# A hybrid decoder layer on one core: GELU moved to VectorE and ScalarE, memory fills one unit earlier, w_out multiplied by branch halves, every other sort step written backwards

## The chip, the cores and the metric

One core of a Trainium2 chip. The metric is device time in microseconds, the median of several runs. TensorE is called PE, VectorE DVE, ScalarE ACT, GpSimd POOL and SyncE SP, as in the profile.

## The reference, cut to what matters

A layer on 512 tokens of width 1024, all in float32. Its first part is what the change touches:

```
z = rmsnorm(h) @ W_in                     # -> u_ssm | q | k | v, 512 columns each
y = S5(u_ssm) + d_skip * u_ssm;  y = gelu(y)          # tanh form
y_ssm = rmsnorm(y * sigmoid(y @ w_glu)) * g_ssm
y_att = rmsnorm_per_head(differential attention of q, k, v: 4 heads, causal)
h = h + concat(y_ssm, y_att) @ W_out
h = h + CrossAttn(rmsnorm(h), rmsnorm(mem))           # 256 memory tokens
h = h + MoE(rmsnorm(h))                               # 64 experts, top 8, and a shared one
return rmsnorm(h)
```

## The kernel before, in words

The program is written by engine: each engine has its own list in order, and semaphores join them. Tokens are four tiles of 128 (`NT`). PSUM has eight banks of 128x512.

*Differential attention* runs in 16 units `u` (`NU`), query tile `u // 4` and head `u % 4`; a unit has `u // 4 + 1` key tiles. PE runs `turn_weights(u)` (L950, transposes of the weights), `scores(u + 2)` (L940), a fill if there is one, and `values(u)` (L960). DVE runs `weights(u)` (reciprocal, L1883, and the scalar_tensor_tensor L1886 that combines the two softmaxes) and `row_max(u + 2)` (mask add, L1874). ACT runs `exps(u + 1)` (L1425), the copy of the turned weights (L1452), and after each fourth unit `outputs` (squares and a copy of the four heads). Scores have two pairs of banks (0 to 3), turned weights banks 4 and 5, outputs bank 6, fills bank 7.

*Fills.* Keys and values of the cross-attention memory come from 16 small products. Four run ahead of the S5 output; `fill(0)` to `fill(11)` stand in units 0 to 11, each 16 matmul instructions of 256 columns (L896 keys, L909 values), evicted by `mem_out` on ACT in the next unit (L1403, L1407). `fill(4)` and `fill(8)` each begin new weight blocks.

*GELU* runs on POOL (L2260 to L2267) on all four tiles at once, 128x2048: two steps for y + d_skip u, three for the inner polynomial, then ACT's tanh in unit 10 (`TANH_AT`, L1449), then two more steps. When the units are over, PE turns the GELU (L992, 16 transposes), ACT evicts (L1459), PE multiplies by w_glu (L766, `dense`), ACT takes the sigmoid (L1462), DVE multiplies (L1608), ACT squares and takes the root, DVE scales (L1915), PE turns both branches together (L747), ACT and DVE evict with the gains (L1311, L1660), and PE multiplies by w_out in two column halves of two row blocks each. DVE adds the result to h (L1611, `residual`).

*Weights* outside the experts are 1 MB blocks in the three buffers `dw`, loaded by SP in the order of `blocks`; block i waits until block i - 3 is used up (`release`). Experts 0 and 1, three blocks of 1 MB each, are queued on SP behind the second block of wq_x.

*The sort.* `slot_table` draws an expert's row numbers, eight at a time, in 16 steps of MAX8 and MATCH_REPLACE8 on 64 partitions, and writes them with a stride of four into groups of 32 slots. A slot is a partition of the gathers and scatters in the expert stage; an empty one moves nothing.

## Time and profile before

| what | value |
|---|---|
| median of 3 runs | 1190.99 us (1184.29 to 1196.14) |
| profiled execution | 1187.29 us |
| its span | 1185.5 us, 13271 instructions |
| PE busy | 1096.1 us, 92% |
| DVE, ACT, POOL busy | 391.1, 232.0, 147.6 us |
| granted PE clock over the span | 0.967 of full speed |

Durations come from this one execution. A line number is one of the kernel before. A matmul in float32 is recorded as two instructions, so a block product of 16 matmuls is counted as x32. A time in brackets is the idle time of the engine before the row, with what ended it.

### The profile page before, as it was taken

How to read it: one execution, taken by the hardware profiler on the slowest of the kernel's cores; microseconds unless marked ns; L12 is line 12 of the kernel's file. 1: busy time of each engine (PE TensorE's matmuls, PEld its weight loads, DVE VectorE, ACT ScalarE, POOL GpSimd, SP SyncE). 2: the span in 40 equal slices, each digit the busy share in tenths (PEclk: the TensorE clock that was granted, in tenths of full speed). 3: DMA queues.
4: the chain of work that ended last, by engine and by line, in shares of the span. 5: the costliest groups of instructions: out<-in, count | busy, mean ns of one | idle time of the engine just before them, and what ended most of it. 6: DMA issues, size and time to landing. Idle time of an engine off the chain costs nothing.

```text
span 1185.5 us, 13271 instructions
## 1 busy us (share of the span) xinstructions
PE 1096.1 (92%) x5059; PEld 527.9 (45%) x5059; DVE 391.1 (33%) x899; ACT 232.0 (20%) x525; POOL 147.6 (12%) x194
## 2 busy tenths in 40 slices
PE   7999797977799987999999999999899999999996
PEld 4444585754444454444444443333234334443332
DVE  1983565353202012016932222212122121111147
ACT  3311432334202023003101111111011111111142
POOL 3000005120000000000022121221121212121100
PEclk9999798988899998999999999999899999999998
DMA  7225322212127240223469999999999999999996
GB/s 217 99 71 106 67 103 50 77 65 71 36 71 283 72 177 1 68 71 132 192 245 413 421 421 420 420 421 420 421 420 421 419 422 419 421 420 419 413 418 258
DMA packets 77346, 298.82 MB, mean 252 GB/s; under 512 B 20342, under 2 KB 23707, under 8 KB 50652
## 3 DMA queue, kind: packets, MB, share of 16 engines
q1 hardware_dynamic: 64386, 264.29, 56.8%
q0 software_dynamic: 12672, 33.57, 7.2%
q8 instruction: 42, 0.69, 0.2%
q14 instruction: 28, 0.23, 0.1%
q10 hardware_dynamic: 218, 0.04, 0.0%
HBM read 280.04 MB, written 27.39 MB: 259 GB/s over the span
## 4 chain that ended last, share of the span: by engine, by line
PE 84%; DVE 8%; DMA 4%; ACT 3%; issue 1%; SPq 0%; DVEq 0%; POOL 0%; POOLq 0%
PE ps L1167 26%; PE ps L766 26%; PE ps L1183 13%; PE ps L1149 4%; PE ps L896 2%; PE ps L909 2%; DMA dw<-expert_rows 2%; PE ps L747 2%; PE ps L1048 1%; PE ps L1024 1%; PE ps L1191 1%; DVE z L2059 1%; DVE z L1886 1%; PE ps L940 1%; DVE z L2056 1%
## 5 line engine op out<-in xcount | busy, mean ns | idle before, releaser
L1167 PE MATMUL ps<-ring,z 128*32 128x512 f32 (+2 forms) x1056 | 285.7, 597 | 1.0 <-DVE z L2107 1.0
L766 PE MATMUL ps<-dw,act_t 128*128 128x512 f32 x576 | 250.3, 595 | 1.8 <-ACT act_t L1311 0.9
L766 PEld LDWEIGHTS ps<-dw,act_t 128*128 128x128 f32 x576 | 109.4, 191 | 137.9 <-issue 136.4
L1183 PE MATMUL ps<-ring,act_t 128*32 128x512 f32 (+2 forms) x528 | 145.3, 596 | 0.9 <-DVE act_t L2132 0.9
L1167 PEld LDWEIGHTS ps<-ring,z 128*32 128x32 f32 (+2 forms) x1056 | 90.3, 131 | 111.0 <-issue 108.7
L1167 PE MATMUL ps<-dw,z 128*64 128x512 f32 (+2 forms) x256 | 99.0, 594 | 0.3 <-DVE z L2107 0.3
L1167 PE MATMUL ps<-z 128*32 128x512 f32 (+2 forms) x288 | 87.8, 628 | 4.0 <-issue 4.0
L1540 ACT ACTIVATE tok<-ps 128x256 f32<-128x256 f32 x44 | 16.9, 384 | 305.4 <-PE ps L1167 305.4
L2087 DVE COPY z<-ps 128x512 f32<-128x512 f32 x44 | 30.5, 692 | 117.6 <-PE ps L1183 117.6
L1183 PEld LDWEIGHTS ps<-ring,act_t 128*32 128x32 f32 (+2 forms) x528 | 43.4, 131 | 49.2 <-issue 47.0
L2273 POOL COPY ixb<-tabs 128x1 uint32<-128x1 uint32 x88 | 17.1, 194 | 376.2 <-DVE z L2087 362.9
L1608 DVE TENSOR_TENSOR tok<-tok,ps 128x256 f32<-128x256 f32 x22 | 9.3, 422 | 156.3 <-ACT tok L1540 156.3
L1608 DVE TENSOR_TENSOR act_t<-tok,ps 128x256 f32<-128x256 f32 x22 | 9.3, 422 | 148.1 <-ACT tok L1540 148.1
L766 PE MATMUL ps<-act_t,dw 128*128 128x512 f32 x128 | 55.2, 593 | 0.9 <-ACT act_t L1311 0.9
L1183 PE MATMUL ps<-act_t 128*64 128x512 f32 (+2 forms) x128 | 50.9, 597 | 2.8 <-issue 2.8
L1536 ACT ACTIVATE z<-ps 128x512 f32<-128x512 f32 x44 | 26.3, 597 | 134.3 <-PE ps L1183 134.3
L1611 DVE TENSOR_TENSOR h<-h,ps 128x512 f32<-128x512 f32 x24 | 16.2, 686 | 103.6 <-PE ps L766 101.0
L2317 POOL DMA_INDIRECT expert_rows<-z,ixb x44 | 44.8, 1018 | 36.8 <-POOL ixb L2273 34.5
L1167 PEld LDWEIGHTS ps<-z 128*32 128x32 f32 (+2 forms) x288 | 26.7, 133 | 42.4 <-issue 41.6
L1183 PE MATMUL ps<-dw,act_t 128*32 128x512 f32 (+2 forms) x144 | 43.6, 596 | 0.0
L1149 PEld LDWEIGHTS ps<-cst,tok 128*128 128x128 f32 x264 | 32.6, 193 | 24.3 <-issue 24.3
L1167 PEld LDWEIGHTS ps<-dw,z 128*64 128x64 f32 (+2 forms) x256 | 28.9, 130 | 28.2 <-issue 27.6
(327 smaller groups left out, 1251.0 us busy)
## 6 DMA issues: line engine op xcount, KB each, us to landing
ring<-in_w_gate SPq DMA_DIRECT2D x42, 1024.0 KB
ring<-in_w_up SPq DMA_DIRECT2D x42, 1024.0 KB
ring<-in_w_down SPq DMA_DIRECT2D x42, 1024.0 KB, 28.3
dw<-in_w_gate SPq DMA_DIRECT2D x11, 1024.0 KB
dw<-in_w_up SPq DMA_DIRECT2D x11, 1024.0 KB
act_t<-in_w_down SPq DMA_DIRECT2D x11, 1024.0 KB, 28.9
z<-in_w_gate SPq DMA_DIRECT2D x11, 1024.0 KB, 22.8
z<-in_w_up SPq DMA_DIRECT2D x11, 1024.0 KB, 26.9
```

The lines of the kernel that those rows point to most:

```text
L747: ins = pe.transpose(ps[:, c, i * P:(i + 1) * P], src[:, i, c * P:(c + 1) * P], ident)
L766: ins = pe.matmul(ps[0:m, bank0 + j, 0:n], lhs(w, q * 4 + c4, c4, j), rhs(w, q * 4 + c4, c4, j), start=(q == 0 and c4 == 0), stop=(q == le ...
L896: ins = pe.matmul(ps[:, bank, 0:MEM], w4(dw[:, i % 3, :])[:, c4, j * P:(j + 1) * P], memt[:, hf * 4 + c4, :], start=(hf == 0 and c4 == 0), ...
L909: ins = pe.matmul(ps[:, bank, 0:256], memt[:, hf * 4 + c4, m * P:(m + 1) * P], w4(dw[:, i % 3, :])[:, c4, n * 256:(n + 1) * 256], start=(h ...
L1149: ins = pe.transpose(ps[:, c // 4, (c % 4) * P:(c % 4 + 1) * P], xg[r % 4][:, c:D:NC_D], ident)
L1167: ins = pe.matmul(ps[rows, 2 + r % 2, :], xtt[r % 2][:, c, rows], ring_wgu(BUF[x])[:, :, c, :], start=(c == 0), stop=(c == NC_D - 1))
L1183: ins = pe.matmul(ps[rows, 5 + n, :], htt[r % 2][:, c, rows], ring_wd(BUF[x])[:, c, n * 512:(n + 1) * 512], start=(c == 0), stop=(c == 1))
L1536: act.activation(yo[j % 2][:, 0:512], ps[:, 5, :], ACT.Copy).then_inc(e_yea, 1)
L1608: return dve.tensor_tensor(o, a, b, ALU.mult)
L2087: dve.tensor_copy(yo[j % 2][:, 512:D], ps[:, 6, :]).then_inc(e_yev, 1)
L2273: pool.tensor_copy(ixb[:, b:b + 1], tabs[:, which, col:col + 1] if isinstance(col, int) else tabs[:, which, bass.ds(col, 1)]).then_inc(s_p ...
L2317: pool.indirect_dma_start(yr, bass.IndirectOffsetOnAxis(ap=ixb[:, b:b + 1], axis=0), yo[r % 2], None, bounds_check=last_row, oob_is_err=Fa ...
```

## The change

GELU leaves POOL. DVE computes y + d_skip u tile by tile in units 2 to 5 (`gelu_input`), ACT squares it (units 3 to 6), DVE forms the inner product (units 5 to 8), ACT takes tanh (units 6 to 9), DVE forms twice the GELU (units 7 to 10). PE turns it in four steps in units 11 to 14 by way of bank 7 (`turn_gelu`), ACT evicts with the factor 0.5 behind each. `fill(0)` runs before unit 0, `fill(u + 1)` in unit u. The w_out blocks are ordered by branch: attention rows first, both column halves, then the SSM rows. The attention half is turned and multiplied without waiting for the SSM norm; the SSM half is turned unnormalized, and 1/rms, one number per token, is applied when its product is added to h. Each of the four block products ends in a semaphore step of its own, and a weight block is released when it ends. In `slot_table` each odd step writes its eight values in the opposite order. POOL's `s_gst` steps in the expert stage use another semaphore.

```diff
@@ -48,7 +48,7 @@
 LAMBDA0 = 0.8 - 0.6 * math.exp(0.0)
 BIG = 1e30
 K_EARLY = 4
-TANH_AT = 10
+GELU_SQUARE_AT, GELU_TANH_AT, GELU_TURN_AT = 3, 6, 16 - K_EARLY - 1
 GELU_C = math.sqrt(2.0 / math.pi)
 TWO_PI = 2.0 * math.pi
@@ -298,7 +298,10 @@
     half_blocks("wv_x", 2)
     blocks.append(("w_glu", 0, 0, [(lambda v: v.rearrange("p (c n) -> p c n", c=4),
                                     t["w_glu"][0].rearrange("(c p) n -> p c n", p=P))]))
-    half_blocks("w_out", 2)
+    for part, rows in enumerate((slice(SW, D), slice(0, SW))):
+        for cb in range(2):
+            src = t["w_out"][0][rows, cb * 512:(cb + 1) * 512].rearrange("(c p) n -> p c n", p=P)
+            blocks.append(("w_out", part, cb, [(lambda v: v.rearrange("p (c n) -> p c n", c=4), src)]))
     half_blocks("wq_x", 2)
     half_blocks("wo_x", 2)
     for hf in range(2):
...
@@ -456,7 +459,7 @@
     for name, cb, hf, _ in blocks:
         if name in ("wk_x", "wv_x"):
             release.append((s_kv, 4 * cb + (8 if name == "wv_x" else 0) + 4))
-        elif hf == 0 and (name, cb, 1) in index:
+        elif name != "w_out" and hf == 0 and (name, cb, 1) in index:
             firsts += 1
             release.append((dw_half, firsts))
         else:
@@ -976,37 +979,65 @@
         scores(1)
         pe.wait_ge(s_yea, 2)
         pe.wait_ge(s_yev, 2)
+        def turn_gelu(c):
+            if c == 0:
+                pe.wait_ge(s_kve, 16)
+                pe.wait_ge(s_yg, NT)
+            else:
+                pe.wait_ge(s_yge, c)
+            for i in range(NT):
+                ins = pe.transpose(ps[:, 7, i * P:(i + 1) * P], gl[0][:, i, c * P:(c + 1) * P], ident)
+            ins.then_inc(s_ygt, 1)
+        fill(0)
         for u in range(NU):
             turn_weights(u)
             if u + 2 < NU:
                 scores(u + 2)
-            if u < 16 - K_EARLY:
-                fill(u)
+            if u + 1 < 16 - K_EARLY:
+                fill(u + 1)
+            elif u - GELU_TURN_AT < 4:
+                turn_gelu(u - GELU_TURN_AT)
             values(u)
-        pe.wait_ge(s_yg, 1)
-        pe.wait_ge(s_e, 2 * NU)
-        for c in range(4):
-            for i in range(NT):
-                ins = pe.transpose(ps[:, c, i * P:(i + 1) * P], gl[0][:, i, c * P:(c + 1) * P], ident)
-            ins.then_inc(s_ygt, 1)
         pe.wait_ge(s_yge, 4)
         pe.wait_ge(s_wte, NU)
-        pe.wait_ge(s_oe, NT)
-        dense([("w_glu", 0, 0)], 4, NT, lambda w, c, c4, j: ygt[:, c, j * P:(j + 1) * P], weight_rhs, s_gl)
+        dense([("w_glu", 0, 0)], 4, NT, lambda w, c, c4, j: ygt[:, c, j * P:(j + 1) * P], weight_rhs, s_gl,
+              bank_waits=[[], [], [(s_oe, NT)], []])
+        def turn_half(bank0, src, ready):
+            for c in range(4):
+                for i in range(NT):
+                    if c == 0:
+                        pe.wait_ge(ready, i + 1)
+                    ins = pe.transpose(ps[:, bank0 + c, i * P:(i + 1) * P], src[:, i, c * P:(c + 1) * P], ident)
+                ins.then_inc(s_tf, 1)
+        def out_part(part, cb, bank0, bank_waits=()):
+            dense([("w_out", part, cb)], bank0, NT, lambda w, c, c4, j: at3[:, 4 * (1 - part) + c4, j * P:(j + 1) * P],
+                  weight_rhs, s_wo, bank_waits=bank_waits)
+        pe.wait_ge(s_e, 2 * NU)
+        turn_half(0, tok3[:, :, SW:D], s_cat)
+        pe.wait_ge(s_tea, 6)
+        pe.wait_ge(s_tev, 6)
+        out_part(0, 0, 0)
         pe.wait_ge(s_sg, NT)
-        pe.wait_ge(s_kve, 16)
-        turn(s_tf, NT, tok3, lambda c, i: [(s_cat, i + 1)] if c == 0 else [])
+        turn_half(4, gl[2], s_y3)
+        out_part(0, 1, 0, [[(s_h1, j + 1)] for j in range(NT)])
         pe.wait_ge(s_tea, 8)
         pe.wait_ge(s_tev, 8)
-        for cb in range(2):
-            dense([("w_out", cb, 0), ("w_out", cb, 1)], 4 * cb, NT, tokens_lhs, weight_rhs, s_wo)
-        turn(s_tf, NT, h, lambda c, i: [(s_h1, c + 4)] if c % 4 == 0 and i == 0 else [])
+        out_part(1, 0, 0, [[(s_h1, NT + j + 1)] for j in range(NT)])
+        out_part(1, 1, 4)
+        turn(s_tf, NT, h, lambda c, i: [(s_h1, 12 + c)] if c % 4 == 0 and i == 0 else [])
         pe.wait_ge(s_tea, 12)
         pe.wait_ge(s_tev, 12)
         for cb in range(2):
@@ -1438,35 +1469,50 @@
         exps(0)
         for u in range(NU):
-            if 1 <= u <= 16 - K_EARLY:
-                mem_out(K_EARLY + u - 1, 7)
             if u + 1 < NU:
                 exps(u + 1)
+            if u < 16 - K_EARLY:
+                mem_out(K_EARLY + u, 7)
             if u % HEADS == 0 and u:
                 outputs(u // HEADS - 1)
-            if u == TANH_AT:
-                act.wait_ge(s_gin, 1)
-                act.activation(gl[2], gl[1], ACT.Tanh, scale=GELU_C).then_inc(s_th, 1)
+            if 0 <= u - GELU_SQUARE_AT < NT:
+                i = u - GELU_SQUARE_AT
+                act.wait_ge(s_gin, i + 1)
+                act.activation(gl[1][:, i, :], gl[0][:, i, :], ACT.Square, scale=math.sqrt(0.044715)).then_inc(s_gst, 1)
+            if 0 <= u - GELU_TANH_AT < NT:
+                i = u - GELU_TANH_AT
+                act.wait_ge(s_gin, NT + i + 1)
+                act.activation(gl[2][:, i, :], gl[1][:, i, :], ACT.Tanh, scale=GELU_C).then_inc(s_th, 1)
             act.wait_ge(s_wtf, u + 1)
             n = (u // HEADS + 1) * P
             act.activation(wt[:, u % 2, 0:u // HEADS + 1, :],
                            ps[:, 4 + u % 2, 0:n].rearrange("p (j q) -> p j q", q=P), ACT.Copy).then_inc(s_wte, 1)
+            if 0 <= u - GELU_TURN_AT < 4:
+                c = u - GELU_TURN_AT
+                act.wait_ge(s_ygt, c + 1)
+                act.activation(ygt[:, c, :], ps[:, 7, :], ACT.Copy, scale=0.5).then_inc(s_yge, 1)
         outputs(NT - 1)
         roots(3, slice(16, 32), slice(68, 84))
-        for c in range(4):
-            act.wait_ge(s_ygt, c + 1)
-            act.activation(ygt[:, c, :], ps[:, c, :], ACT.Copy).then_inc(s_yge, 1)
         for i in range(NT):
             act.wait_ge(s_gl, i + 1)
             act.activation(gl[1][:, i, :], ps[:, 4 + i, :], ACT.Sigmoid).then_inc(s_sg, 1)
+        act.wait_ge(s_pce, 2)
+        def turned_half(first, bank0, chunk0):
+            for c in range(0, 4, 2):
+                act.wait_ge(s_tf, first + c + 1)
+                act.activation(at3[:, chunk0 + c, :], ps[:, bank0 + c, :], ACT.Copy, scale=gcat[:, chunk0 + c:chunk0 + c + 1]
+                               ).then_inc(s_tea, 1)
+        turned_half(8, 0, 4)
         squares(0, NT, gl[2], gl[3], SW, [[(s_y3, i + 1)] for i in range(NT)])
+        turned_half(12, 4, 0)
         roots(4, slice(0, NT), slice(8, 8 + NT))
-        act.wait_ge(s_pce, 2)
-        turned(8, gcat, S, at3)
         turned(16, pcol[:, R_GX:R_GX + 8], S, at3)
-        squares(0, NT, h, tok3, D, [[(s_h1, 8)]] + [[]] * 3)
+        squares(0, NT, h, tok3, D, [[(s_h1, 16)]] + [[]] * 3)
         roots(5, slice(0, NT), slice(8, 8 + NT))
         for q in range(0, 8, 2):
             act.wait_ge(s_qx, q + 1)
@@ -1886,12 +1932,35 @@
             dve.scalar_tensor_tensor(out=e[0], in0=e[1], scalar=r, in1=e[0], op0=ALU.mult, op1=ALU.add
                                      ).then_inc(s_w, 1)
+        def gelu_input(i):
+            if i == 0:
+                dve.wait_ge(s_yt, 16 * (2 * NT + 1))
+                dve.wait_ge(s_y, 4)
+            link(mul(gl[0][:, i, :], z3[:, i, 0:SW], dsk))
+            add(gl[0][:, i, :], gl[0][:, i, :], y3[:, i, :]).then_inc(s_gin, 1)
+        def gelu_inner(i):
+            dve.wait_ge(s_gst, i + 1)
+            dve.scalar_tensor_tensor(out=gl[1][:, i, :], in0=gl[1][:, i, :], scalar=1.0, in1=gl[0][:, i, :],
+                                     op0=ALU.add, op1=ALU.mult).then_inc(s_gin, 1)
+        def gelu_twice(i):
+            dve.wait_ge(s_th, i + 1)
+            dve.scalar_tensor_tensor(out=gl[0][:, i, :], in0=gl[2][:, i, :], scalar=1.0, in1=gl[0][:, i, :],
+                                     op0=ALU.add, op1=ALU.mult).then_inc(s_yg, 1)
         row_max(0)
         row_max(1)
         for u in range(NU):
             weights(u)
             if u + 2 < NU:
                 row_max(u + 2)
+            for step, first in ((gelu_input, 2), (gelu_inner, 5), (gelu_twice, 7)):
+                if 0 <= u - first < NT:
+                    step(u - first)
         dve.wait_ge(s_osq, NU)
         r0, rstd2, var = st2[:, 0:16], st2[:, 16:32], st[:, 16:32]
@@ -1903,18 +1972,22 @@
         dve.wait_ge(s_oe, NT)
         for i in range(NT):
             o = tok3[:, i, SW:D].rearrange("p (h d) -> p h d", h=HEADS)
-            mul(o, o, rstd2[:, 4 * i:4 * i + 4].unsqueeze(2).to_broadcast([P, HEADS, P]))
-        dve.wait_ge(s_yg, 1)
+            mul(o, o, rstd2[:, 4 * i:4 * i + 4].unsqueeze(2).to_broadcast([P, HEADS, P])).then_inc(s_cat, 1)
+        dve.wait_ge(s_yg, NT)
         for i in range(NT):
             dve.wait_ge(s_sg, i + 1)
-            mul(gl[2][:, i, :], gl[0][:, i, :], gl[1][:, i, :]).then_inc(s_y3, 1)
-        dve.wait_ge(s_sq, 10)
-        rstd(4, st[:, 0:NT], SW, st[:, 8:8 + NT], st2[:, 0:NT])
-        for i in range(NT):
-            dve.tensor_scalar(tok3[:, i, 0:SW], gl[2][:, i, :], st2[:, i:i + 1], None, ALU.mult).then_inc(s_cat, 1)
-        turned(8, gcat, S, at3)
+            dve.scalar_tensor_tensor(out=gl[2][:, i, :], in0=gl[0][:, i, :], scalar=0.5, in1=gl[1][:, i, :],
+                                     op0=ALU.mult, op1=ALU.mult).then_inc(s_y3, 1)
+        def turned_half(first, bank0, chunk0):
+            for c in range(1, 4, 2):
+                dve.wait_ge(s_tf, first + c + 1)
+                dve.tensor_scalar(at3[:, chunk0 + c, :], ps[:, bank0 + c, :], gcat[:, chunk0 + c:chunk0 + c + 1], None, ALU.mult
+                                  ).then_inc(s_tev, 1)
+        turned_half(8, 0, 4)
         def residual(filled, ready, first=0, bank=lambda n: n):
             for n in range(first, first + 8):
@@ -1923,7 +1996,28 @@
                 dve.wait_ge(filled, n + 1)
                 add(hh, hh, ps[:, bank(n), :]).then_inc(ready, 1)
-        residual(s_wo, s_h1)
+        def attention_part(cb):
+            for i in range(NT):
+                hh = h[:, i, cb * 512:(cb + 1) * 512]
+                dve.wait_ge(s_wo, 4 * cb + i + 1)
+                add(hh, hh, ps[:, i, :]).then_inc(s_h1, 1)
+        attention_part(0)
+        turned_half(12, 4, 0)
+        dve.wait_ge(s_sq, 10)
+        rstd(4, st[:, 0:NT], SW, st[:, 8:8 + NT], st2[:, 0:NT])
+        attention_part(1)
+        for cb in range(2):
+            for i in range(NT):
+                hh = h[:, i, cb * 512:(cb + 1) * 512]
+                dve.wait_ge(s_wo, 8 + 4 * cb + i + 1)
+                if cb == 0:
+                    dve.wait_ge(s_h1, i + 1)
+                else:
+                    dve.wait_ge(s_h1, NT + i + 1)
+                dve.scalar_tensor_tensor(out=hh, in0=ps[:, 4 * cb + i, :], scalar=st2[:, i:i + 1], in1=hh,
+                                         op0=ALU.mult, op1=ALU.add).then_inc(s_h1, 1)
         turned(16, pcol[:, R_GX:R_GX + 8], S, at3)
@@ -2047,13 +2141,14 @@
             for q in range(SLOTS // 8):
                 k, row = divmod(q, 4)
                 eight = ts_[0:NE, k * QW + row:(k + 1) * QW:4]
+                filled = eight if q % 2 == 0 else ts_[0:NE, k * QW + row + QW - 4:k * QW + row - 1:-4]
                 left = tv[0:NE, :] if q else values
                 if between and q in between:
                     shared_hidden(between.index(q))
                 if q == ids_at:
                     dve.wait_ge(s_srf, 1)
                     dve.tensor_copy(eid[:], ps[0:1, 0, 2 * NE:3 * NE]).then_inc(s_tab, 1)
-                link(dve.max(out=eight, in_=left))
+                link(dve.max(out=filled, in_=left))
                 if ids_at is not None and q == 0:
                     dve.wait_ge(s_ord, 1)
                 ins = dve.match_replace(out=tv[0:NE, :], in_to_replace=eight,
@@ -2246,26 +2341,6 @@
         pool.memset(toep, 0.0).then_inc(s_zero, 1)
-        gsteps = [0]
-        def link(ins):
-            gsteps[0] += 1
-            ins.then_inc(s_gst, 1)
-            pool.wait_ge(s_gst, gsteps[0])
-        fg = [v.rearrange("p i d -> p (i d)") for v in gl]
-        pool.wait_ge(s_yt, 16 * (2 * NT + 1))
-        pool.wait_ge(s_y, 4)
-        link(pool.tensor_tensor(gl[0], z3[:, :, 0:SW], dsk.unsqueeze(1).to_broadcast([P, NT, SW]), ALU.mult))
-        link(pool.tensor_tensor(fg[0], fg[0], y3.rearrange("p i d -> p (i d)"), ALU.add))
-        link(pool.tensor_tensor(fg[1], fg[0], fg[0], ALU.mult))
-        link(pool.tensor_scalar(fg[1], fg[1], 0.044715, 1.0, ALU.mult, ALU.add))
-        pool.tensor_tensor(fg[1], fg[1], fg[0], ALU.mult).then_inc(s_gin, 1)
-        pool.wait_ge(s_th, 1)
-        link(pool.tensor_scalar(fg[2], fg[2], 0.5, 0.5, ALU.mult, ALU.add))
-        pool.tensor_tensor(fg[0], fg[0], fg[2], ALU.mult).then_inc(s_yg, 1)
         last_token, last_row = pool.to_reg(S - 1), pool.to_reg(S * TOPK - 1)
         def index_of(b, which, col, n):
...
...
```

## Rows read from the trace of the kernel before

**Rows 1.** Busy time by stage: stretch, us, then each engine's busy us (instructions)

```profile
190.00:272.00 82.00, 66.55 (x318) 50.49 (x318) 42.23 (x60) 28.66 (x105) 25.42 (x7) 0.92 0.21 75
...
595.00:1135.00 540.00, 531.51 (x2848) 213.18 (x2843) 109.79 (x252) 68.85 (x131) 106.94 (x174) 0.99 1.00 412
```

**Rows 2.** Timeline of DVE: start us, us, line, operation

```profile
187.32 0.35 DVE L1886 SCALAR_TENSOR_TENSOR z<-z,st 128x128 f32<-128x128 f32 x1
...
196.44 4.67 DVE L1886 SCALAR_TENSOR_TENSOR z<-z,st 128x128 f32<-128x128 f32 x1
...
253.22 4.96 DVE L1886 SCALAR_TENSOR_TENSOR z<-z,st 128x384 f32<-128x384 f32 x1
```

**Rows 3.** Timeline of POOL

```profile
191.88 4.50 POOL L2260 TENSOR_TENSOR ring<-z 128x2048 f32<-128x2048 f32 x1 [180.65 <-DMA z<-in_d_skip]
...
253.27 4.50 POOL L2267 TENSOR_TENSOR ring<-ring 128x2048 f32<-128x2048 f32 x1
```

**Rows 4.** Timeline of PE in the attention units

```profile
184.99 0.30 PE L950 MATMUL ps<-cst,z 128*128 128x128 f32 x1 [2.72 <-DVE z L1886]
...
201.16 0.48 PE L950 MATMUL ps<-cst,z 128*128 128x128 f32 x1 [5.59 <-DVE z L1886]
...
217.55 1.99 PE L909 MATMUL ps<-dw,ring 128*128 128x256 f32 x8 [2.08 <-DMA dw<-in_wv_x]
...
225.93 3.72 PE L909 MATMUL ps<-dw,ring 128*128 128x256 f32 x16
...
258.24 0.90 PE L950 MATMUL ps<-cst,z 128*128 128x128 f32 x3 [4.01 <-DVE z L1886]
```

**Rows 5.** Finer stretches; PEclk is the granted clock

```profile
186.00:191.00 5.00, 5.00 (x20) 4.24 (x19) 1.50 (x5) 0.02 (x1) 0.00 (x0) 0.74 0.82 186
...
201.00:208.00 7.00, 6.84 (x24) 5.13 (x24) 3.92 (x6) 0.37 (x2) 6.79 (x3) 0.67 0.01 2
...
258.20:266.50 8.30, 8.26 (x29) 5.69 (x30) 2.70 (x5) 0.89 (x3) 0.00 (x0) 0.67 0.00 0
266.50:277.00 10.50, 6.34 (x39) 3.80 (x37) 6.22 (x13) 7.38 (x24) 0.00 (x0) 1.00 0.59 201
277.00:283.00 6.00, 5.22 (x23) 4.82 (x24) 0.31 (x1) 1.00 (x5) 0.00 (x0) 0.53 0.00 0
```

**Rows 6.** The chain of waits in unit 13, which has no fill

```profile
271.13 0.66 PE ps L950 x4
...
273.36 1.22 DVE st L1874
...
274.95 0.76 DVE z L1886
275.75 0.67 PE ps L950 x4
```

**Rows 7.** Timeline of PE from the last unit to w_out

```profile
282.40 2.77 PE L992 MATMUL ps<-cst,ring 128*128 128x128 f32 x16
287.80 15.56 PE L766 MATMUL ps<-dw,ring 128*128 128x512 f32 x32 [2.63 <-ACT ring L1459]
309.63 6.48 PE L747 MATMUL ps<-cst,tok 128*128 128x128 f32 x32 [6.27 <-DVE tok L1915]
317.00 55.17 PE L766 MATMUL ps<-dw,act_t 128*128 128x512 f32 x128 [0.89 <-ACT act_t L1311]
```

**Rows 8.** Timelines of ACT and DVE behind the gate matmuls

```profile
303.40 0.60 ACT L1462 ACTIVATE ring<-ps 128x512 f32<-128x512 f32 x1 [2.84 <-PE ps L766]
...
304.03 0.69 DVE L1608 TENSOR_TENSOR ring<-ring 128x512 f32<-128x512 f32 x1 [2.74 <-ACT ring L1462]
...
315.28 1.62 DVE L1660 TENSOR_SCALAR act_t<-ps,gcat 128x512 f32<-128x512 f32 x2 [0.72 <-PE ps L747]
```

**Rows 9.** DMA issues between 100 and 380 us, median us to landing

```profile
dw<-in_w_out SPq DMA_DIRECT2D x4, 1024.0 KB, 5.2
```

**Rows 10.** Queues, from the page: packets, MB, share of 16 engines

```profile
q0 software_dynamic: 12672, 33.57, 7.2%
```

12 lines of the change are left out of this document (6 added, 6 removed).

## The prediction

> **What bounds the kernel now.** I first read the busy time by stage. From 595 us on TensorE is busy 531.51 of 540 us [rows 1]; the change edits nothing there but the row numbering of the sort, so what happens earlier can only shift this stage. The attention stage, 190 to 272 us, is where something is to be had: PE is busy 66.55 of 82 us at a granted clock of 0.92 [rows 1]. The chain of waits and the timelines say why.
>
> First, VectorE stalls while GpSimd runs the GELU. The 128x128 scalar_tensor_tensor of `weights` takes 0.35 us at 187.32, but 4.67 us at 196.44, and the 128x384 one takes 4.96 us at 253.22 [rows 2]. GpSimd's 4.5 us operations start at 191.88 and 253.27 [rows 3], beside them. PE waits for exactly these: 5.59 us before 201.16 and 4.01 us before 258.24. A third wait, 2.72 us before 184.99, is the first softmax unit's plain latency, with the K/V fill queued behind it [rows 4]. Each wait is followed by matmuls at the low level of the clock: the stretches of 5, 7 and 8.3 us after them ran at 0.74, 0.67 and 0.67 [rows 5]. A fill at full speed is 16 instructions in 3.72 us [rows 4].
>
> Second, the last four units carry no fill and run by latency: turn at 271.13, next at 275.75, 4.62 us apart, of which the row maximum alone is 1.22 [rows 6].
>
> Third, between the last value matmul and cross-attention there are serial steps with PE idle: the GELU turns at 282.40 and their evictions before the gate matmuls at 287.80, then squares, a root, a scaling and turns between the gate's end (287.80+15.56=303.36) and the start of w_out at 317.00, with 6.27 us idle before the turns at 309.63 [rows 7].
>
> **The change, part by part.**
>
> *GELU off GpSimd.* Removed: two PE waits, 5.59+4.01=9.6 us [rows 4], and the slow clock behind them, 7x(1-0.67)+8.3x(1-0.67)=5.0 us [rows 5]. Added on VectorE: per token tile a multiply and an add (units 2 to 5), and two scalar_tensor_tensors (units 5 to 8 and 7 to 10), 16 operations of 128x512 at 0.69 each by the gate product [rows 8], 11 us in all; on ScalarE four squares and four tanhs of 0.6 (the sigmoid, same shape) [rows 8]. They lie ahead of the next unit's `weights` in VectorE's order, so what is queued behind them is PE's next turn. A unit with a fill lasts about 5 us, and the fill now sits ahead of that turn. The widest unit gives the upper end of the loop: 4.62 us from turn to turn with one key tile more than most [rows 6], of which row maximum and `weights` shrink with the key tiles (1.22 and 0.76 at four of them, 0.35 for `weights` at one [rows 2, 6]). With three tiles or two I estimate 3.7 and 3.0 us, with one or two GELU steps (1.4 or 1.5) 4.4 to 5.2, against PE's 4.4 to 5.7 (a 3.72 fill and turn, scores and values); only unit 5, with input and inner product together (2.2), overruns, by 0.4. ScalarE's additions stand ahead of the weight copy that `values` needs, but a 3.72 us fill covers them; if it were gone each would cost 0.6. The input of the first step (y3 and d_skip) landed when GpSimd started, 191.88 [rows 3]; VectorE comes to it at about 196, so no wait. Part: -14.6+0.4 = -14.2.
>
> *Fills forward by one.* Fill 0 (3.7) goes into the 2.72 us wait and keeps the clock up: 2.72 removed, and 5x(1-0.74)=1.3 behind it [rows 4, 5]. In return unit 11 loses its fill and becomes a latency unit of about 4.3 us with 2.1 us of PE work: +2.2. Its first K/V value block is still requested when fill 3 ends, and the half-fill that waited 2.08 us at 217.55 [rows 4] waits as long. Part: -1.8.
>
> *GELU turns inside units 11 to 14.* 16 transposes, four in each unit, in idle PE time (2.77 us for all at the slow clock [rows 7]); they queue after the scores, so the latency loop does not contain them. Bank 7 is free once the last fill is evicted. The gate matmuls then start right after the last values: 282.4 becomes the start instead of 287.80 [rows 7], -5.3. Against it stands the clock. The unfilled units held 1.00 until 277.00 and then fell to 0.53 [rows 5]; there are now five such units instead of four, with somewhat more PE work in each. I take 1.2 us for it, between 0 (the extra work holds the clock) and 5 (all five at half speed, 1.7 per unit for turn and scores, less what was already slow). The gate matmuls took 15.56 us with a slow start, 16 of the same at full speed take 55.17/4=13.8 [rows 7]; I take 15.3. Part: -5.3+1.2-0.3 = -4.4.
>
> *w_out by branch halves.* Before, from the gate's end to the end of w_out: 317.00+55.17-303.36=68.8 us [rows 7]. After: the attention half is normalized behind the gate matmuls (VectorE's chain after the last unit needs some 7 us, the gate 15), its turns follow the gate directly. On the path now are the last sigmoid 0.60, the gate product 0.69 and two evictions on VectorE 1.62, with gaps 3.2 us in all, because these stand in that order on VectorE [rows 8]; PE's first 16 turns run inside that (32 took 6.48 at the slow clock [rows 7]; I take 1.9 for 16 at full speed, where 3.2 is the other end). Then four parts of 13.8 and the second 16 turns, 1.9: 3.2+55.2+1.9=60.3, so -8.5. SSM's squares, root and 1/rms lie beside the first two parts (27.6 us, against the 6.27 of idle time that they cost before [rows 7]) and are applied in the residual's scalar_tensor_tensor, four per half as before. New waits: part two writes banks 0 to 3 again, each after an add of 0.7 that comes while other banks are filled; no cost. On SP the third weight block waits for the gate and is needed 3.2+13.8+1.9+13.8=32.7 us later, the fourth for part one and is needed 1.9+27.6=29.5 us later; a block lands in 5.2 us [rows 9]. wq_x's first two blocks wait for parts two and three, and the six megabytes of experts still go behind the second of them, ahead of wq_x's third; that one is requested at the end of w_out as before, and needed some 30 us later. No cost.
>
> *Odd sort steps reversed.* Same instructions. Empty slots of the last group of eight no longer lie at the high positions alone. Some 64 rows per expert are 8 per position, give or take half a row: 6% of the share of the software queue, 7.2% of 1185 us [rows 10], so 5 us of work on an uneven DMA engine, which PE, busy 531.51 of 540, hides [rows 1]: 0, between -5 and +5. The Trainium skill ("DMA: Bandwidth & Descriptors", The descriptor swizzle) assigns groups of four partitions to engines, which would make the high positions engines 7 and 15; its section "Latency and other measured facts" calls these two usually slower, so that the reversal would give them more work. By that the term would be positive; no row here separates engines.
>
> *Sum.* -14.2-1.8-4.4-8.5 = -28.9 us. The stages behind start earlier with the same queues, so nothing is given back. The profiled execution took 1187.3 us for a span of 1185.5, which gives 1158.4. It lay 3.7 under the median of the runs, 1190.99; against that the sum gives **1162**. I state 1161.
>
> **The rivals.**
> *A, VectorE becomes the bound of the filled units.* My slack there is under half a microsecond in units 2, 7 and 8. If gaps and semaphores add 0.7 to each of nine units, 6 us come back: 1168. For it: the sums are close to PE's. Against: in 190 to 272 VectorE was busy 42.23 of 82 us, stalls included [rows 1].
> *B, more comes back than I count.* Clock held through the unfilled units (-1.2), full-speed gate (-1.5), and a more even DMA stage (-5): 1154.
> *C, slower than before: the low clock stays.* The price is 13.8 us for each of the five gate and w_out blocks: five at half speed cost 69, so over 29 us of low-level excess (about 60 us at the low level) undoes the sum; all five would give about 1230. For it: five latency units ahead. Against: after 6.27 us idle the turns at 309.63 ran slow and w_out at full speed directly after, 55.17 us, and the gate needed no more than 1.8 us of excess [rows 7].
> *D, the high DMA engines cannot take the work.* Then the reversal adds what I took as 5 us of uneven work where it hurts, and PE would start to wait for weights: 1166. For it: DMA's share of that stage is 1.00 too [rows 1]. Against: PE loses only 8.5 of 540 us there to waits of every kind [rows 1]. The page for this is the one named at the sort.
> *E, the change doesn't do what it says:* PE's stalls in attention weren't GpSimd's doing, and the scalar_tensor_tensors stay long. Then only w_out's 8.5, the start of the gate and fill 0 remain, about 15: 1176. Against it: the short and long instructions are the same code [rows 2], and the long ones stand beside GpSimd's [rows 3].
>
> **How the numbers follow.** Forecast 0.57, A 0.15, B 0.17, C 0.02, D 0.03, E 0.04, 0.02 for what I don't see. The single runs of before spread over 12 us, so 1% (12 us) is about what a measurement here can tell from no change. The clock term reaches 1.2 below and 3.8 above, the sort 5 either way, and the profile's relation to the median 4: from B's 1154 less 3 to A's 1168 plus 4, **1151 to 1172**. Faster by over 1% needs under 1179: forecast, A, B, D and most of E, 0.95. Within 1%: 0.03. Slower: 0.02.
>
> **What the profile of the changed kernel would show.** No scalar_tensor_tensor of `weights` above 0.8 us and no PE wait over 2.5 us between the first unit and the last; fills all near 3.7. Turns of units with a fill 4.4 to 5.7 apart: if 6, A is right. The gate's first matmul at about 267 and right behind the last values; w_out's first at the gate's end + 3.2; cross-attention's turns at about 343. The expert stage as long as before, 540 us to within 5. The forecast is wrong if the stages up to 343 come as said and the expert stage is longer, or if the unfilled units run at 6 us each.

## The result, and the profile after

The changed kernel takes 1153.31 us (median of 4 runs, 1152.35 to 1157.5), the kernel before 1191.17 (4 runs, 1184.29 to 1196.14). The ratio is 0.9714, 95% interval 0.9676 to 0.9752: 34 us faster by the ratio, 37.9 by the two medians, where 29 were forecast. 1153.3 lies inside the stated 1151 to 1172, close to its lower end. The profiled execution took 1152.35 us for a span of 1150.6, 34.9 under the span of before.

First the timeline of DVE in the changed kernel, in unit 5, the one with the most GELU steps: mask add and row maximum, input (L1654, L1657), inner product (L1946), then `weights` of unit 6.

```profile
197.09 0.35 DVE L1932 SCALAR_TENSOR_TENSOR z<-z,st 128x128 f32<-128x128 f32 x1
...
211.13 0.43 DVE L1657 TENSOR_TENSOR ps<-ps,cst 128x256 f32<-128x256 f32 x1 [1.61 <-PE ps L943]
...
212.21 0.68 DVE L1654 TENSOR_TENSOR ring<-z 128x512 f32<-128x512 f32 x1
212.92 0.69 DVE L1657 TENSOR_TENSOR ring<-ring 128x512 f32<-128x512 f32 x1
213.53 0.68 DVE L1946 SCALAR_TENSOR_TENSOR ring<-ring 128x512 f32<-128x512 f32 x1
...
214.58 0.48 DVE L1932 SCALAR_TENSOR_TENSOR z<-z,st 128x256 f32<-128x256 f32 x1
```

Against [rows 2]: the 128x128 operation is back at 0.35, and none of the 16 exceeds 0.75 us. A GELU operation of 128x512 takes 0.68, as the gate product did.

Then the timeline of PE from the first fill to the last quarter of w_out.

```profile
180.95 3.69 PE L899 MATMUL ps<-ring,dw 128*128 128x256 f32 x16 [0.19 <-issue]
184.47 0.27 PE L953 MATMUL ps<-cst,z 128*128 128x128 f32 x1
...
203.08 1.99 PE L912 MATMUL ps<-dw,ring 128*128 128x256 f32 x8 [2.34 <-DMA dw<-in_wv_x]
...
215.12 0.44 PE L953 MATMUL ps<-cst,z 128*128 128x128 f32 x2
...
250.39 0.65 PE L953 MATMUL ps<-cst,z 128*128 128x128 f32 x4 [1.65 <-DVE z L1932]
...
264.24 13.90 PE L769 MATMUL ps<-dw,ring 128*128 128x512 f32 x32
277.98 1.91 PE L1018 MATMUL ps<-cst,tok 128*128 128x128 f32 x16
280.92 13.97 PE L769 MATMUL ps<-dw,act_t 128*128 128x512 f32 x32 [1.03 <-ACT act_t L1506]
294.73 1.91 PE L1018 MATMUL ps<-cst,ring 128*128 128x128 f32 x16
```

The reader is to see, against [rows 4]: no wait for DVE before unit 0 (184.47) nor above 1.65 us later (250.39, the longest); the wait for the first value block is still there, 2.34. Unit 6 starts at 215.12, when `weights` ended (214.58+0.48=215.06): this is the unit that overruns, by 0.1. The gate starts at 264.24 with no wait and takes 13.90, against 287.80 and 15.56 [rows 7]; between its last matmul and w_out there are 16 turns and 1.03 us of idle time, against 6.27 and 0.89 [rows 7], and the second 16 turns stand between w_out's first part and the other three (41.37).

The granted clock in finer stretches of the changed kernel (PEclk is the third number from the end):

```profile
222.00:230.00 8.00, 6.15 (x24) 4.79 (x25) 3.11 (x7) 2.57 (x13) 0.00 (x0) 0.79 0.72 254
245.00:255.00 10.00, 7.20 (x45) 4.68 (x44) 5.48 (x11) 6.65 (x21) 0.00 (x0) 1.00 0.58 211
255.00:264.00 9.00, 6.63 (x46) 5.04 (x47) 3.83 (x8) 4.64 (x11) 0.00 (x0) 1.00 0.00 0
264.00:278.00 14.00, 14.00 (x37) 6.30 (x36) 6.29 (x17) 6.20 (x15) 0.00 (x0) 1.00 0.00 0
```

Against [rows 5]: the unfilled units, now five, ran at 1.00 to their end. The only low stretch left in the attention units follows the wait for the second value block.

Cross-attention's first projections, right behind the turns, and the last down product, from the chain of waits (start us, us, what):

```profile
337.85 3.07 PE ps L750 x28
...
1100.37 3.67 PE ps L1214 x16
```

Cross-attention's turns start at 337.68 instead of 372.0, 34.3 us earlier, and the difference stays nearly whole: the first gate/up matmul of the expert stage is at 570.84 instead of 604.08, 33.2 earlier, and the last down product starts at 1100.37 instead of 1135.50, 35.1 earlier.

### The profile page after: what moved, and what is told of

It reads as the page before. It is cut to its first block, busy times and chain, and to the rows that moved or that the text cites. A ratio compares the mean times of both kernels' runs of the same rounds, so it can differ in the third digit from the quotient of the medians.

```text
span 1150.6 us, 13301 instructions
## 1 busy us (share of the span) xinstructions
PE 1081.7 (94%) x5059; PEld 517.3 (45%) x5059; DVE 388.6 (34%) x919; ACT 235.9 (21%) x532; POOL 121.4 (11%) x187
## 4 chain that ended last, share of the span: by engine, by line
PE 86%; DVE 6%; DMA 4%; ACT 2%; issue 1%; SPq 0%; DVEq 0%; POOL 0%; POOLq 0%
PE ps L1198 27%; PE ps L769 26%; PE ps L1214 14%; PE ps L1180 4%; PE ps L899 2%; PE ps L912 2%; DMA dw<-expert_rows 2%; PE ps L1079 1%; PE ps L1222 1%; PE ps L1055 1%; DVE z L2154 1%; PE ps L750 1%; DVE z L2151 1%; DMA dw<-in_wv_x 1%; PE ps L943 1%
## 5 line engine op out<-in xcount | busy, mean ns | idle before, releaser
L1654 DVE TENSOR_TENSOR tok<-tok,ps 128x256 f32<-128x256 f32 x22 | 9.3, 421 | 155.9 <-ACT tok L1586 155.9
L1654 DVE TENSOR_TENSOR act_t<-tok,ps 128x256 f32<-128x256 f32 x22 | 9.3, 421 | 148.1 <-ACT tok L1586 148.1
L1657 DVE TENSOR_TENSOR h<-h,ps 128x512 f32<-128x512 f32 x24 | 16.3, 686 | 75.7 <-PE ps L769 71.4
## 6 DMA issues: line engine op xcount, KB each, us to landing
act_t<-in_w_down SPq DMA_DIRECT2D x11, 1024.0 KB, 28.9
```

The source lines that it names most:

```text
L1654: return dve.tensor_tensor(o, a, b, ALU.mult)
```

## The experiments

Twelve runs, one of them the changed kernel again. To compare traces I use four lengths: A, from the first scores to the start of the gate matmuls; B, from the start of the gate to the end of w_out; E, from the first gate/up matmul to the start of the last down product of the expert stage; L, from the same first gate/up matmul to PE's last four matmul instructions, which sum expert rows. The start of the first scores varies from 179.9 to 181.6 us in kernels that are the same up to there, so it is left out of A. Between w_out and the expert stage no kernel differs, and yet this stretch takes 229.7 to 234.5 us; spans of single traces carry that too. Each ratio is to runs of the kernel before made beside that kernel (their medians were 1185.6 to 1191.2 us), so it is not the quotient with the first row.

| kernel | median us | ratio to before (95%) | A | B | E | L |
|---|---|---|---|---|---|---|
| before | 1191.17 | 1 | 106.2 | 84.4 | 531.4 | 569.8 |
| changed | 1153.31 | 0.9714 (0.9676 to 0.9752) | 84.2 | 73.6 | 529.5 | 567.7 |
| the same again | 1154.23 | 0.9729 (0.9713 to 0.9745) | 84.0 | 73.6 | 529.2 | 567.5 |
| GELU moved, alone | 1172.66 | 0.9888 (0.984 to 0.9935) | 91.3 | 84.4 | 531.8 | 569.9 |
| old w_out | 1161.44 | 0.9787 (0.9745 to 0.9829) | 82.3 | 82.8 | 531.7 | 567.3 |
| late turn | 1162.52 | 0.98 (0.9757 to 0.9843) | 92.9 | 73.7 | 529.8 | 567.9 |
| late turn, PE kept busy | 1160.33 | 0.9787 (0.977 to 0.9803) | 90.7 | 75.4 | 529.6 | 567.6 |
| old fills | 1152.78 | 0.9713 (0.9668 to 0.9758) | 84.5 | 73.6 | 529.4 | 567.7 |
| old sort | 1156.36 | 0.975 (0.9705 to 0.9795) | 84.1 | 73.6 | 531.5 | 569.7 |
| three early products | 1153.94 | 0.9722 (0.9677 to 0.9768) | 89.3 | 73.6 | 531.4 | 567.4 |
| no fill in unit 3 | 1151.91 | 0.9715 (0.9698 to 0.9731) | 82.3 | 73.6 | 529.4 | 567.7 |
| additions on GpSimd | one run, 1167.61 | - | 99.1 | 73.6 | 529.5 | 567.5 |
| memsets on GpSimd | one run, 1152.37 | - | 84.2 | 73.6 | 531.3 | 567.5 |
| VectorE padded | one run, 1158.74 | - | 91.7 | 73.6 | 531.4 | 567.5 |

**The same again.** No edit.

> The changed kernel once more, unedited, with a trace of its own: which differences between stages of two traces mean nothing. Expected: the start of the gate within 1.5 us of the first trace's, the expert stage (first gate/up matmul to the start of the last down product) within 2 us of its 529.5.

Gate at 264.79 (first trace 264.24), E 529.2. Both as expected. In this trace the half-fill (8 matmul instructions) after the first value block ran partly at the low clock and the one after the second did not; in the first trace it was the other way round:

```profile
203.71 3.13 PE L912 MATMUL ps<-dw,ring 128*128 128x256 f32 x8 [2.26 <-DMA dw<-in_wv_x]
```

In old w_out, whose attention stage is the same, neither was slow, and A is 82.3. So such luck is worth up to 2 us in A.

**GELU moved, alone.** The kernel before with GELU moved, shown shortened; as in the change, PE's wait for the copied heads also stands at the third bank of the gate and no longer ahead of it:

```diff
-        (POOL: seven GELU operations of 128x2048)
+        (DVE: gelu_input, gelu_inner, gelu_twice; ACT: Square and Tanh per tile, as in the change)
-        pe.wait_ge(s_yg, 1)
+        pe.wait_ge(s_yg, NT)
```

> The kernel before with one part of the change: GELU on VectorE and ScalarE, tile by tile; fills, GELU turns, w_out and sort as before. My theory (GpSimd's operations block VectorE, and PE's two long waits and the slow clock behind them come from that): no scalar_tensor_tensor above 0.8 us, no PE wait of 4 us or more between units, 14 us less than before, a span near 1171 and a ratio near 0.988. Rival (the stalls are not GpSimd's doing): long instructions and waits stay, ratio 1.00. Rival (VectorE becomes the bound): the units with a fill are longer than 5.2 us and the gain is under 8.

The span is 1170.3, the ratio 0.9888, A falls by 14.9 us. PE's timeline in this kernel:

```profile
184.07 0.30 PE L950 MATMUL ps<-cst,z 128*128 128x128 f32 x1 [2.72 <-DVE z L1894]
...
184.73 3.72 PE L896 MATMUL ps<-ring,dw 128*128 128x256 f32 x16
...
266.61 1.91 PE L994 MATMUL ps<-cst,ring 128*128 128x128 f32 x16
271.97 3.55 PE L766 MATMUL ps<-dw,ring 128*128 128x512 f32 x4 [3.44 <-ACT ring L1466]
```

The two long waits of [rows 4] are gone. The first unit's wait, 2.72, is not, but the fill behind it takes 3.72 and not 5.00: the low clock that I had put down to that wait (0.74 in [rows 5]) does not come with it by rule. This luck flatters the 14.9 by 1.3 us; a half-fill behind the second value block, 3.43 here and 1.99 in the kernel before, takes 1.4 back. The GELU turns and their evictions still stand open, 5.36 us from 266.61 to 271.97.

**Additions, and memsets, on GpSimd.** The changed kernel with work for POOL that nobody needs, on a spare 128x2048 stretch `spare`:

```diff
+        spare = view(ringf, 56 * K, 2048)
...
+        pool.memset(spare, 0.0).then_inc(s_zero, 1)
+        pool.wait_ge(s_zero, 4)
+        for n in range(7):
+            pool.tensor_tensor(spare, spare, spare, ALU.add).then_inc(s_zero, 1)
+            pool.wait_ge(s_zero, n + 5)
```

```diff
+        for n in range(18):
+            pool.memset(spare, 0.0).then_inc(s_zero, 1)
+            pool.wait_ge(s_zero, n + 4)
```

> The changed kernel plus seven additions of 128x2048 on GpSimd on a spare stretch of SBUF, nobody's input, from about 189 us on, some 28 us in all (one wait of PE before the gate, long fulfilled, orders them before the weights that overwrite the stretch). Theory (GpSimd operations that read SBUF block VectorE operations with two SBUF inputs): scalar_tensor_tensors of weights up to 4.7 us, PE waits of 2 to 5 us and low clock in units 1 to 7, 8 to 15 us more than the changed kernel. Rival (the stalls of before came from the data dependence on GELU or from its DMA): no instruction stretched, span as the changed kernel's.

> The changed kernel plus 18 memsets of 128x2048 on GpSimd on the same spare stretch, some 33 us in all: GpSimd as busy as in the run with additions, but it reads nothing. If only reading GpSimd operations block VectorE's two-input operations: no stretched instruction, span as the changed kernel's within 1.5 us. If any busy GpSimd blocks them: as with the additions, each VectorE operation up to 1.8 us long, since a memset is that short.

The additions: POOL's timeline, then DVE's beside it, then PE's.

```profile
193.25 26.97 POOL L2350 TENSOR_TENSOR ring<-ring 128x2048 f32<-128x2048 f32 x7
...
195.47 0.69 DVE L1921 TENSOR_REDUCE st<-ps 128x2 f32<-128x512 f32 x1
...
197.43 3.97 DVE L1658 TENSOR_TENSOR ring<-ring 128x512 f32<-128x512 f32 x1
201.33 0.15 DVE L1929 RECIPROCAL st<-st 128x1 f32<-128x1 f32 x1
201.51 3.36 DVE L1930 SCALAR_TENSOR_TENSOR st<-st 128x1 f32<-128x1 f32 x1
204.91 3.77 DVE L1933 SCALAR_TENSOR_TENSOR z<-z,st 128x128 f32<-128x128 f32 x1
...
208.74 0.48 PE L953 MATMUL ps<-cst,z 128*128 128x128 f32 x1 [9.92 <-DVE z L1933]
```

The row maximum (one input, PSUM) and the reciprocal (one input) keep their time in the midst of it; everything with two SBUF inputs is stretched, the 128x1 scalar_tensor_tensor from 0.22 to 3.36. The mask add (L1658 on 128x256, one input in PSUM) kept its 0.43 too. PE waits 9.92 us, and A is 14.9 longer than in the changed kernel. That moving the GELU had saved the same 14.9 is chance: the additions fall on other units. The memsets:

```profile
191.14 33.47 POOL L2348 MEMSET ring<- 128x2048 f32 x18 [179.91 <-DMA z<-in_d_skip]
...
201.92 0.22 DVE L1930 SCALAR_TENSOR_TENSOR st<-st 128x1 f32<-128x1 f32 x1
202.17 0.48 DVE L1933 SCALAR_TENSOR_TENSOR z<-z,st 128x256 f32<-128x256 f32 x1
```

33 us of busy POOL and not one stretched operation. The additions differ from the memsets in more than reading: they have two inputs and last twice as long. The trace of the kernel before settles that. Its two one-input POOL operations took 1.90 us, as long as a memset (33.47/18=1.86), and stretched VectorE all the same; this is the second of them, with the operation beside it:

```profile
251.29 1.90 POOL L2266 TENSOR_SCALAR ring<-ring 128x2048 f32<-128x2048 f32 x1 [40.06 <-ACT ring L1449]
...
251.75 1.44 DVE L1883 SCALAR_TENSOR_TENSOR st<-st 128x1 f32<-128x1 f32 x1
```

VectorE's 0.22 became 1.44, ending where POOL's operation ends (253.19). So the cause is not the dependence on GELU, not its DMA and not a busy POOL, but POOL operations that read SBUF. It is what the Trainium skill states ("SBUF — State Buffer", SBUF: two separate sides): the shared port pair is an exclusive lock between a GpSimd operation that reads SBUF and a VectorE operation with two SBUF inputs. The traces agree: a stretched operation ends with POOL's or a little later, as at 258.18 beside 257.77 [rows 2, 3], and the one-input reciprocal kept 0.15. The runs with additions and with memsets are single ones; the stretched operations, 1.3 to 4.0 us instead of 0.22 to 0.69, leave no doubt of the effect.

**VectorE padded.** The changed kernel with three more multiplications per unit:

```diff
+            if 2 <= u <= 10:
+                for n in range(3):
+                    dve.tensor_tensor(view(ringf, (58 + 2 * n) * K, 512), view(ringf, 56 * K, 512), view(ringf, 56 * K, 512), ALU.mult)
```

> The changed kernel plus three multiplications of 128x512 on VectorE (2.05 us) in each of units 2 to 10, ahead of the GELU steps, on a spare stretch that nobody reads. It measures the slack of VectorE in these units. By the changed kernel's timeline weights(u+1) ends 0.5, 3.0, 0.6, 0, 1.0, 3.6, 0.5, 1.1 and 0.8 us before PE needs it in units 2 to 10; so PE should lose 9 to 10 us, up to 14 with the clock. Rival (VectorE's work is hidden with room to spare): under 3 us. Rival (queueing makes it worse than one for one): over 16 us.

A grew by 7.5 us instead of 9 to 10. PE waited for `weights` 1.24, 0.30, 1.14, 1.75, 1.20, 0.59 and 0.86 us, 7.1 in all, and the first of these was taken back by the wait for the weight block behind it, which shrank from 2.34 to 0.80. The one at 218.84, the longest, has the low clock behind it:

```profile
203.10 1.99 PE L912 MATMUL ps<-dw,ring 128*128 128x256 f32 x8 [0.80 <-DMA dw<-in_wv_x]
...
218.84 0.44 PE L953 MATMUL ps<-cst,z 128*128 128x128 f32 x2 [1.75 <-DVE z L1932]
...
220.25 5.17 PE L912 MATMUL ps<-dw,ring 128*128 128x256 f32 x16
```

Nine units had 2.05 us more work each, 18.5 in all, and 7.5 came through: VectorE had slack for more than half of it. Rival A charged 6 us for 0.7 per unit, which is 6.3 in all; with three times that added, length A grew by 7.5 only, so its price was too high.

**Old fills.** The changed kernel with the fills at their old place (shortened; ScalarE evicts them in the old order too, and `GELU_TURN_AT` is one higher):

```diff
-        fill(0)
         for u in range(NU):
...
-            if u + 1 < 16 - K_EARLY:
-                fill(u + 1)
+            if u < 16 - K_EARLY:
+                fill(u)
```

> The changed kernel with the K/V fills where they were (fill u in unit u, none ahead of unit 0), and the GELU turned one unit later, in units 12 to 15. Theory: the first unit waits 2.7 us again with the low clock behind it (1.3), and one latency unit of 2.2 us of waiting goes: 2 us more than the changed kernel. Rival (with the GELU steps on VectorE the old order, in which ScalarE's exponentials stand behind the fill's eviction, no longer keeps up): units with a fill over 5.5 us, 6 us more or worse.

No difference that can be told: ratio 0.9713 against 0.9714 and 0.9729, A 84.5 against 84.2 and 84.0.

```profile
184.34 0.30 PE L953 MATMUL ps<-cst,z 128*128 128x128 f32 x1 [2.72 <-DVE z L1931]
...
185.00 3.72 PE L899 MATMUL ps<-ring,dw 128*128 128x256 f32 x16
```

The wait of 2.72 is back, and one latency unit with 2.2 us of waiting is gone: 0.5 us by rows, 0.3 measured, which is less than the luck of the clock. My other 1.3, the low clock behind the first wait, did not come: this fill took 3.72.

**Three early products.** `K_EARLY = 3`, no other edit.

> The changed kernel with one early K/V product fewer (K_EARLY 3): three ahead of the S5 output, 13 fills, GELU turned in units 12 to 15. The scan's result was ready at 166.1 us in the changed kernel and the fourth product ended at 169.4, so 3.3 us go there; the fill that unit 11 now carries lengthens it from 4.5 to some 5.7 us. Theory: 2 us less than the changed kernel, span near 1148.5, ratio near 0.970. Rival (the added fill delays the clock or a weight block more): no less than the changed kernel.

Refuted, by a queue that I had not followed. The first scores did come 2.5 us earlier (177.53), but the second weight block of fill 1 goes into a buffer that is free only when the fourth key product is done, and that product is now fill 0:

```profile
187.32 3.67 PE L899 MATMUL ps<-ring,dw 128*128 128x256 f32 x8 [2.67 <-DMA dw<-in_wk_x]
```

2.67 us of waiting and 1.68 of low clock; the gate starts at 266.80, later than in the changed kernel. The median, 1153.94, is the same as the changed kernel's (1153.31 and 1154.23).

**Late turn, and late turn with PE kept busy.** The changed kernel with the GELU turned in one piece behind unit 15 and evicted there; the second also has four transposes of the identity in each of units 11 to 14:

```diff
-            elif u - GELU_TURN_AT < 4:
-                turn_gelu(u - GELU_TURN_AT)
+            elif u - GELU_TURN_AT < 4:         # second kernel only
+                pe.wait_ge(s_kve, 16)
+                for i in range(NT):
+                    pe.transpose(ps[:, 7, i * P:(i + 1) * P], ident, ident)
```

> The changed kernel with the GELU turned in one piece behind the last unit, as before, by way of banks 0 to 3. Theory: turns and evictions stand open again before the gate, 5 us, and the idle time puts the gate's first matmuls on the low clock, 1.4 us more: the gate starts 5 us later and takes 15.3 us instead of 13.9, in all 6.5 us more than the changed kernel, span near 1157. Rival (the four turns inside the units are what holds the clock there, more than the serial step costs): units 12 to 15 themselves slow down and it is 9 us or more. Rival (the turns are hidden either way): under 3 us.

> The kernel with the GELU turned behind the last unit, plus four throwaway transposes of the identity in each of units 11 to 14, in the place where the changed kernel turns the GELU; nobody reads them. It separates the two gains of the interleaved turns. Theory (PE work in the gaps holds the clock): granted clock 1.00 from unit 11 to the last values, where the late turn had 0.83 and 0.67, and the 16 late turns in 1.9 us instead of 3.6; the serial 5.4 us between the last values and the gate stay. Span some 2 to 4 us under the late turn's 1158.1 and 5 over the changed kernel's. Rival (the low clock there was chance, or came from the slow weight block before): clock no better than 0.9 in those units, or no difference from the late turn.

Late turn, last units and gate, then its clock; then the same of the kernel with throwaway work.

```profile
268.07 3.62 PE L998 MATMUL ps<-cst,ring 128*128 128x128 f32 x16
273.47 1.98 PE L769 MATMUL ps<-dw,ring 128*128 128x512 f32 x4 [1.78 <-ACT ring L1488]
...
248.00:258.00 10.00, 6.65 (x30) 3.64 (x29) 5.29 (x10) 5.49 (x19) 0.00 (x0) 0.83 0.51 192
```

```profile
266.13 1.91 PE L1002 MATMUL ps<-cst,ring 128*128 128x128 f32 x16
271.49 15.70 PE L769 MATMUL ps<-dw,ring 128*128 128x512 f32 x32 [3.45 <-ACT ring L1492]
...
245.00:258.00 13.00, 10.20 (x62) 6.67 (x62) 6.65 (x14) 7.03 (x23) 0.00 (x0) 1.00 0.47 163
258.00:266.50 8.50, 6.14 (x40) 5.31 (x39) 3.29 (x7) 2.81 (x7) 0.00 (x0) 0.80 0.00 0
```

Late turn costs 6.5 us of span over the mean of the two traces of the changed kernel, and 8.3 and 9.2 in the medians. The 6.5 matches the theory by luck, since the stretch between w_out and the experts, where nothing differs, was 2.4 shorter in this trace. From the first scores to the end of the gate the late turn takes 106.9 us (A, and the gate), the busy kernel 106.4, the changed one 98.1 and 97.9. The late turn's 8.9 are 5.4 between the last values and the gate (268.07 to 273.47) and 3.5 of low clock in the units before: both the theory's step and the rival's are there.

The throwaway work kept the clock at 1.00 to 258 us, where the late turn had 0.83, but it fell in the last two units (0.80), and the gate then took 15.70 where the late turn had 14.00. The busy kernel's 8.4 are 5.4 of the serial step, 1.8 of the gate's clock and 1.2 in the last units; its span, 1158.4, is no shorter than the late turn's 1158.1. So half of that theory fell. To the last unit PE had as many transposes in the same places as in the changed kernel, whose clock stayed at 1.00. With the real turns it fell once too, for the values at 262.29 in the kernel with three early products (1.98 us instead of 1.16). That the clock held through the last units is therefore partly chance. What the turns inside the units do secure is that nothing stands between the values and the gate. The gate took 13.90 in all ten traces in which it follows the values without a wait; in the four in which it waits for the GELU it took 15.56, 15.57, 14.00 and 15.70.

**Old w_out.** The changed kernel with `residual`, one `turn` of both branches and column halves as before.

> The changed kernel with w_out as before (two column halves, both branches turned after the SSM norm). From the gate's end to the end of w_out the changed kernel takes 59.7 us, the one before 68.8. Theory: the 9.1 us come back whole, since nothing behind depends on it: span near 1160, ratio to before near 0.978. Rival (the loads of wq_x or of the experts hide or enlarge it): the difference at the start of the expert stage is under 6 or over 12 us.

```profile
262.79 13.90 PE L766 MATMUL ps<-dw,ring 128*128 128x512 f32 x32
282.95 6.61 PE L747 MATMUL ps<-cst,tok 128*128 128x128 f32 x32 [6.27 <-DVE tok L1956]
290.46 10.11 PE L766 MATMUL ps<-dw,act_t 128*128 128x512 f32 x23 [0.89 <-ACT act_t L1321]
```

B is 9.2 us longer, and the ratio 0.9787 (its interval, 0.9745 to 0.9829, just reaches those of the changed kernel). The span grew only by 6.0 against the first trace of the changed kernel: A was 1.9 shorter by luck of the clock, the stretch between w_out and the experts 1.0 shorter, and the time from the first gate/up matmul to the end 0.8 shorter; the first scores came 0.4 later. The difference at the start of the expert stage is 6.8, inside the theory's bounds.

**Old sort.** `dve.max(out=eight, ...)` in every step.

> The changed kernel with all sort steps written in the same order. Theory: PE paces the expert stage and hides any unevenness of the DMA engines: 0 within 1.5 us, expert stage 540 us as in both kernels. Rival (evenness shortened the stage or the last scatters): up to 5 us longer. Rival (the far engines cannot take the work): up to 5 us shorter.

E is 531.5 against 529.5 and 529.2, ratio 0.975 against 0.9714 and 0.9729, with intervals that overlap. By the table E has two values, and kernels with the new sort are found at both (old w_out 531.7, memsets 531.3). What goes with it is the second of two gaps in which PE waits for nothing that the profile shows. From the chain of waits of the changed kernel, then of old w_out:

```profile
976.65 1.30 issue
```

```profile
981.99 2.81 issue
```

This gap is 1.1 to 1.4 us in the traces with E at 529 and 2.8 to 3.7 in those with 531. What makes the gap was not tried, and E by itself says nothing of the reversal. L does. The end of PE's work waits for a load of expert rows in every trace; first the changed kernel, then old sort:

```profile
1138.54 1.98 PE L1287 MATMUL ps<-ring,act_t 128*128 128x512 f32 x4 [0.48 <-DMA ring<-expert_rows]
```

```profile
1142.07 1.98 PE L1287 MATMUL ps<-ring,act_t 128*128 128x512 f32 x4 [0.48 <-DMA ring<-expert_rows]
```

L is 1138.54-570.84=567.7 us in the changed kernel and 1142.07-572.34=569.7 in old sort. In all eleven traces with the new sort it lies between 567.3 and 567.9, whichever value E has, and in the three with the old one (before, GELU moved alone, old sort) between 569.7 and 569.9. The medians differ the same way, by 3.0 and 2.1. So the reversal is worth 2.0 us, more than the theory's 1.5: where PE is later in the expert stage with the new sort, it waits less for expert rows behind it. That this comes from evener DMA engines, as the rival has it, is not shown, since no view here separates engines.

**No fill in unit 3.** A version that the experiments pointed to (shortened; the evictions follow the fills, and the GELU turns move to units 12 to 15):

```diff
+FILL_IN = {u: u + 1 for u in range(3)} | {u: u for u in range(4, 16 - K_EARLY)}
...
-            if u + 1 < 16 - K_EARLY:
-                fill(u + 1)
+            if u in FILL_IN:
+                fill(FILL_IN[u])
```

> The changed kernel with no fill in unit 3, where the first value block is still on its way; fills 4 to 11 run in units 4 to 11 and the GELU turns in units 12 to 15. In the changed kernel PE waits 2.34 us for that block at 203.08. Theory: unit 3 shrinks from 7.2 us to some 4.3, which is the time of the transfer, and unit 11 takes a fill and grows from 4.5 to 5.7: the gate starts 1.5 to 2 us earlier than in the changed kernel, span near 1149. Rival (the unfilled unit ends on the low clock, or the block still isn't there): gate start unchanged or later.

```profile
202.13 0.53 PE L954 MATMUL ps<-cst,z 128*128 128x128 f32 x2 [2.75 <-DVE z L1933]
...
203.75 4.69 PE L913 MATMUL ps<-dw,ring 128*128 128x256 f32 x16
```

Unit 3 shrank from 7.2 to 4.3 us, as expected; the block was there, but behind the unit's own wait (2.75) came a slow fill (4.69). A went from 84.2 to 82.3, which shows nothing alone: old w_out has 82.3 with the fill in unit 3. In time: 0.9715 against 0.9729 for the changed kernel beside it, intervals overlapping. Its span is the lowest of all (1146.9), but that it is faster than the changed kernel is not shown.

## Why the prediction was right, and where it was off

The steps to cross-attention held, and the gain of 34.3 us up to there against my 28.9 comes from sizes; the step behind it, that PE paces the expert stage and hides the sort, was wrong by 2 us.

- *GELU off GpSimd*, -14.2: measured -14.9 alone. The cause, argued from rows standing side by side, is shown by the additions and memsets. The overrun in unit 5 was 0.1, not 0.4: I had taken the loop of a unit with a single measured point, and scaled it a little too long.
- *Fills forward*, -1.8: measured -0.3, less than the luck of the clock. The wait that goes (2.7) and the latency unit that comes (2.2) were right; the clock term behind the wait (1.3) came from one trace, and two others with the same wait have none of it.
- *GELU turns inside the units*, -4.4: measured -8.9. The serial step is 5.4. The clock term had the wrong sign: I charged 1.2 us for a longer unfilled stretch and gave the gate 15.3; in both traces of the changed kernel the clock held 1.00 to the gate, which took 13.90. The gate's part repeats; the clock in the last units is partly luck, as the kernel with throwaway work shows.
- *w_out by halves*, -8.5: measured -9.2 between kernels (B 82.8 to 73.6); the 3.2 us path from gate to w_out was 278.14 to 280.92, 2.8.
- *Sort*, 0: measured -2.0, inside my 5 either way. The reason I gave for 0 failed: PE does not hide the DMA to the end, where it waits for expert rows. The sign that I drew from engines 7 and 15 did not come.
- The first scores began 1.5 us earlier in the first trace of the changed kernel than in that of before. No edit is there; it belongs to the difference of two traces, and I had no term for it.

Sum of the measured terms up to w_out: 14.9+0.3+8.9+9.2=33.3. Directly, A and B together fell by 32.8; the half microsecond between is within the luck of the clock. With the 1.5 that makes the 34.3 at cross-attention. From there 1.1 are lost before the experts, and 1.7 gained from their first gate/up matmul to the end of the span: 34.9.

The median came out 7.7 us under the stated 1161, more than the 6.0 that the sum fell short. The rest is the step from the profile to the median: I added 3.7 because the profiled execution of before lay that far under 1190.99, but that median was itself high (1185.6 to 1187.1 in the four later sets of runs), and the changed kernel's lies 1.0 over its profiled execution.

Rival B was the nearest to the outcome: its first two terms came true, and 2 of the 5 us of its third. Rival A did not show; the padding says that its price was too high. Rivals C and E were wrong: the clock stayed, and the change did what it says. Rival D had the wrong sign.
